# Feed-forward activation tiles at a pitch of 272 columns in place of 264

## The reference

```python
x = x + swiglu_half_ffn(x, ffn1_norm, ffn1_w_in, ffn1_w_out)
h = rms_norm(x, mix_norm)
proj = h @ w_in                       # RWKV-7 part, attention part, branch gates
...
merged = g_a * (o_a @ w_branch_rwkv) + g_b * (o_b @ w_branch_attn)
x = x + merged @ w_out
x = x + swiglu_half_ffn(x, ffn2_norm, ffn2_w_in, ffn2_w_out)

def swiglu_half_ffn(x, norm_g, w_in, w_out):
    h = rms_norm(x, norm_g)
    gate, up = jnp.split(h @ w_in, 2, axis=-1)
    return 0.5 * ((jax.nn.silu(gate) * up) @ w_out)
```

## Time and profile before

| | |
|---|---|
| median of 3 runs | 2350.49 us |
| the profiled execution's span | 2349.0 us |
| TensorE matmul busy | 2337.7 us, 23152 matmuls |
| TensorE weight load busy | 2305.6 us |
| VectorE busy | 1459.5 us |
| ScalarE busy | 985.4 us |
| GpSimd busy | 88.0 us |
| read from HBM | 415.21 MB, 186 GB/s over the span |

### The profile page before, as it was taken

The page is one execution under the profiler, slowest core; times in us unless marked ns, Lnnn a source line. Parts: engine busy times, 40 slices in busy tenths (PEclk is TensorE's granted clock), DMA queues, the critical chain, the costliest instruction groups (busy, mean ns, idle before and its releaser), DMA issues.

```text
span 2349.0 us, 57542 instructions
## 1 busy us (share of the span) xinstructions
PE 2337.7 (100%) x23152; PEld 2305.6 (98%) x23152; DVE 1459.5 (62%) x2004; ACT 985.4 (42%) x1268; POOL 88.0 (4%) x146
## 2 busy tenths in 40 slices
PE   9999999999999999999999999999999999999999
PEld 8999999999999999999999999999999999999999
DVE  6555455555556678878666767766555555545554
ACT  6333333333334544565222346544343333333333
POOL 0000000000002100000000000120000000000000
PEclk9999999999999999999999999999999999999999
DMA  7666566555555756445323637655555555555555
GB/s 240 202 228 209 182 219 245 179 181 182 182 172 170 236 191 208 155 135 187 104 93 114 217 116 209 220 184 183 179 181 184 180 179 179 187 180 180 182 167 171
DMA packets 124082, 428.27 MB, mean 182 GB/s; under 512 B 14488, under 2 KB 20760, under 8 KB 123424
## 3 DMA queue, kind: packets, MB, share of 16 engines
q1 hardware_dynamic: 117504, 393.49, 51.8%
q0 software_dynamic: 6432, 32.64, 4.2%
HBM read 415.21 MB, written 21.33 MB: 186 GB/s over the span
## 4 chain that ended last, share of the span: by engine, by line
PE 96%; DMA 1%; DVE 1%; ACT 1%; issue 0%; DVEq 0%; SPq 0%; ACTq 0%
PE bank L272 30%; PE bank L273 30%; PE bank L274 30%; PE bank L1257 3%; DMA raw<-in_weights 1%; DVE wlo L245 0%; ACT whi L239 0%; DMA x<-in_x 0%; PE bank L1582 0%; PE bank L1395 0%; PE bank L1299 0%; PE bank L1371 0%; PE bank L1598 0%; PE bank L1388 0%; PE bank L1474 0%
## 5 line engine op out<-in xcount | busy, mean ns | idle before, releaser
L245 DVE TENSOR_TENSOR wlo<-raw,whi 128x1024 fp32r<-128x1024 f32 (+3 forms) x794 | 914.0, 1155 | 603.6 <-ACT whi L239 601.2
L272 PE MATMUL bank<-hhi,whi 128*128 128x264 f32 x4048 | 1163.4, 287 | 3.2 <-DVE wlo L245 2.9
L239 ACT ACTIVATE whi<-raw 128x1024 fp32r<-128x1024 f32 (+3 forms) x794 | 793.3, 1002 | 882.6 <-PE bank L274 864.3
L273 PE MATMUL bank<-hlo,whi 128*128 128x264 f32 x4048 | 1147.4, 283 | 0.0
L274 PE MATMUL bank<-hhi,wlo 128*128 128x264 f32 x4048 | 1146.1, 283 | 0.0
L272 PEld LDWEIGHTS bank<-hhi,whi 128*128 128x128 f32 x4048 | 762.5, 188 | 15.4 <-issue 7.3
L273 PEld LDWEIGHTS bank<-hlo,whi 128*128 128x128 f32 x4048 | 763.0, 188 | 0.9
L274 PEld LDWEIGHTS bank<-hhi,wlo 128*128 128x128 f32 x4048 | 759.2, 188 | 0.0
L272 PE MATMUL bank<-mhi,whi 128*128 128x264 f32 x1408 | 399.5, 284 | 0.0
L274 PE MATMUL bank<-mhi,wlo 128*128 128x264 f32 x1408 | 398.9, 283 | 0.0
L273 PE MATMUL bank<-mlo,whi 128*128 128x264 f32 x1408 | 398.9, 283 | 0.0
(11 more groups left out here) (274 smaller groups left out, 1675.7 us busy)
## 6 DMA issues: line engine op xcount, KB each, us to landing
raw<-in_weights SPq DMA_DIRECT2D x666, 512.0 KB, 3.4
raw<-in_weights SPq DMA_DIRECT2D x64, 384.0 KB, 3.1
out_skv<-in_cache POOLq DMA_DIRECT2D x16, 512.0 KB, 4.5
raw<-in_weights SPq DMA_DIRECT2D x32, 256.0 KB, 3.5
raw<-in_weights SPq DMA_DIRECT2D x32, 192.0 KB, 2.5
side<-stg POOLq DMA_DIRECT2D x18, 132.0 KB, 3.7
gates<-side POOLq DMA_DIRECT2D x1, 2376.0 KB, 14.5
x<-in_x SPq DMA_DIRECT2D x4, 528.0 KB, 6.9
```

Source lines behind the costliest of these rows:

```text
L239: act.activation(whi[:, u % RING, 0:n], raw[:, u % RING, 0:n], ACT.Copy).then_inc(hi_done, 1)
L245: dve.tensor_tensor(wlo[:, s, 0:n], raw[:, s, 0:n], whi[:, s, 0:n].bitcast(F32), ALU.subtract).then_inc(lo_done, 1)
L272: pe.matmul(bank[:, 0:T], hi, xhi[:, k], start=(k == 0), stop=False)
L273: pe.matmul(bank[:, 0:T], hi, xlo[:, k], start=False, stop=False)
```

## The change

The gated activations `mhi` and `mlo` are allocated with 272 columns a tile (`WIDE = T + 8`, 1088 bytes, 17 x 64), of which the first 264 are used. As both start on a multiple of 64 bytes, every tile of them does. Before, every second tile began 32 bytes past one. `mlo` then starts 512 bytes later than before, `gated`, `silu`, `prod` and `sq` 1024 bytes later. Shapes, instructions, semaphores and DMAs stay as they are.

```diff
+WIDE = T + 8
...
-        mhi, mlo = put("mhi", at_mix, [DT, T], F32R), put("mlo", at_mix + DT * tile, [DT, T], F32R)
-        gated, silu, prod = (put(k, at_mix + (2 * DT + 2 * i) * tile, [2, T]) for i, k in enumerate(("gated", "silu", "prod")))
-        sq = put("sq", at_mix + (2 * DT + 6) * tile, [DT, T])
+        wide = 4 * WIDE
+        mhi, mlo = (put(k, at_mix + i * DT * wide, [DT, WIDE], F32R)[:, :, 0:T] for i, k in enumerate(("mhi", "mlo")))
+        at_f = at_mix + 2 * DT * wide
+        gated, silu, prod = (put(k, at_f + 2 * i * tile, [2, T]) for i, k in enumerate(("gated", "silu", "prod")))
+        sq = put("sq", at_f + 6 * tile, [DT, T])
```

## The result

The changed kernel takes 2358.68 us (median of 7 runs, 2356.31 to 2361.04) against 2350.42 us for the one before (7 runs): ratio 1.0035, 95% interval 1.0024 to 1.0046. The forecast was 2347.6 us, with a range of 2341.5 to 2355.0.

A forecast was written before the change was run, and what follows sets the result against it. The prediction took TensorE's back-to-back matmuls as the bound. Median 2350.5 us less 2.9 us in the down projections, other parts costing nothing, gave 2347.6 us, with a range of 2341.5 to 2355.0.

The forecast's parts named there:

- What bounds the kernel: Whole kernel: TensorE, busy 2337.7 of 2349.0 us, sets the end; only the distance between matmuls matters, here 510.57 us of down stretches.
- Step 1: Down projections: pitch 1088 leaves only offsets 64, 128, 192, 0; 4224 matmuls at 0.70 ns less each, 2.9 us less.
- the two pricings: Down-stage tiles priced by their own offset (2.9 us less, offset 192 at 366 ns) or the next operand's (3.9 us, 357 to 360).
- the slower case: Rival for the down stages: bad offsets between moving and weight tiles add 3.3 to 7.2 us; chance 0.13.
- The table in the prediction: Time of a tile's three matmuls by offset mod 256, in the four long down stretches: 356.8 to 370.9 ns.
- The bounds: Down stages: nearer limits on the sum, 8.2 us less (best single offset) to 7.2 us more (branch stages).
- The dear side: Upper limit for the down stages, from the branch stages' 121.64 and 122.57 ns a matmul: 3.3 and 7.2 us more.
- Steps 2 to 4: Moved small tensors cost none; VectorE's writes of mhi and mlo at most 0.35 us; semaphores, DMAs, instructions and order unchanged.
- No effect: Rival: the down-stage cycle is paced by something else, offsets only shift time among neighbours, time stays 2350.5 us; chance 0.20.
- A larger gain: Rival: without tiles off the boundary, down-stage tiles fall toward 119.0 ns a matmul, 7.9 us less, 2342.6; chance 0.25.
- The 35 us: Down stages: up to this much to win if all 8.4 ns above the skill's 112.5 ns a matmul were alignment.
- Slower: Rival: moving-tile and weight reads meet at bad offsets in the down stages, +0.77 to +1.70 ns each, 2353.8 to 2357.7; chance 0.13.

The follow-up runs named there:

- e1: Kernel before with mhi, mlo at pitch 1280, each down stage at one offset (0, 64, 128, 32, 96, 192): 123.33, 120.00, 121.33, 121.67, 120.00, 120.95 ns a matmul.
- e3: Against the kernel before: first part pitch 1088, bases 32 bytes on, 121.67 ns a matmul; second part old tiles, small tensors moved 8192 bytes, 92.82 us a long stretch.
- e2: Kernel before at pitch 1280, mhi/mlo both 160, both 224, then 64/192, 64/128, 64/96, 128/64: 122.22, 126.67, 121.48, 122.22, 120.00, 122.22 ns a matmul.
- e9: Kernel before with mhi and mlo at pitch 1280, offset 64 in all six down stages: 2347.05 us, ratio 0.9987.
- e8: Kernel before with wlo 128 bytes on against whi, and mlo 128, 192, 32 bytes on from mhi at pitch 1056: 2361.11 us.

## Why the prediction was wrong

- *What bounds the kernel.* Right: the span moved by 7.6 us and the down stretches by 7.75.
- *Step 1, the sum.* The step that failed is "if each tile keeps the price of its offset". It was tested before the prediction only on one order, that of `hhi` and `mhi`, which pass through the eight offsets in the same sequence. That both agreed to 0.4 ns showed that the address counts; it could not show that an offset has a price of its own. In the new order all four offsets (64, 128, 192, 0) have other prices (369, 366, 363, 375), and e1 gives three of the four others still (360, 364, 363, 370). Forecast -0.70 ns a matmul, measured +1.83: 7.75 us over 4224 matmuls. The tile that was to choose between the two pricings, offset 192, cost 363 ns and fits neither 366 nor 357 to 360. The long stretches passed the 93.4 us that the prediction had set as the sign of the slower case (94.29).
- *What the trace of before already held.* Its 12-tile stages visit the same offsets, but jump from 160 back to 64 at a block's end. There tile 0 costs 369 ns and tile 8 361, both at offset 64; tiles 3 and 11, both at 160, cost 369 and 363. The timeline of one such block, the first matmuls of tiles 0 and 1, then of tiles 8 and 9 (0.37 and 0.36 us apart, rounded to 10 ns):

```profile
718.63 0.28 PE L272 MATMUL bank<-mhi,whi 128*128 128x264 f32 x1
...
719.00 0.29 PE L272 MATMUL bank<-mhi,whi 128*128 128x264 f32 x1
...
721.54 0.28 PE L272 MATMUL bank<-mhi,whi 128*128 128x264 f32 x1
...
721.90 0.29 PE L272 MATMUL bank<-mhi,whi 128*128 128x264 f32 x1
```

  A price per offset fails there by 8 ns a tile. The table in the prediction was made from the four long stages alone.
- *Small slips in the sum.* 4224 x 0.70 is 2.96, not 2.9. The 69.65 us of a short stretch hold 575 distances, so the mean there is 121.1 ns and not 120.92. Together they would have made the gain 3.2 us in place of 2.9.
- *The bounds.* The dear side was cut too short. The branch stages (+0.77 and +1.70 ns) were taken as its end, and the change went just past, +1.83, though the placements tried later reach from 120.00 to 126.67 ns. The range stopped at 2355.0, in the lower half of the slower case, which had a chance of 0.13.
- *Steps 2 to 4.* Right. The small tensors cost nothing (e3, second part), and `mhi` and `mlo` are written in 297 to 304 and 432 to 436 ns.
- *No effect.* Its reason, a rhythm paced by something that ignores the offsets, is refuted by the spread of e1 and e2. The 16-byte line in the Trainium skill (SBUF — State Buffer, Specifications) doesn't cover this: every placement tried is a multiple of 16.
- *A larger gain.* Wrong for this layout. Where a gain does come, in e9, the cause is not that the tiles off a 64-byte boundary are gone: at offset 96 all are off it, and e1 has 120.00 ns there too. The 35 us that the prediction works out by the Trainium skill (TensorE: Matmul & The Clock Gate, Back-to-back issue gap) were no price for this stream: that section gives its formula for an isolated matmul and says that in a stream with a weight load for each matmul both operations set the spacing. No stream here had a steady mean under 120.00 ns.
- *Slower.* The right rival: sign, place and the part of the weights hold; its price, at most 2357.7 us, fell 1 us short of 2358.68. That moving only the weights takes the change's own layout from 94.29 to 93.00 us a stretch is shown. That the two reads meet in the memory is one reading of it; that a weight load's own pace depends on its address is another, and no run here separates them. The Trainium skill (TensorE: Matmul & The Clock Gate, Step-by-step: what each phase is for) has it that the two operands have independent read ports and loading weights takes nothing from the running matmul. The measured dependence on the weights' address (122.78 to 121.11 ns) speaks against that as a full account, but doesn't refute it while the second reading stands.

So the cause is shown as far as this: the place of `mhi` and `mlo` against the weights, and nothing else that the change moved, made the down stages slower. Left open is the rule by which a cycle of offsets settles into its rhythm. The same cycle gave 122.78, 121.11 and 120.55 ns by where it was entered and where the weights lay, and e8's up stages two values at one placement. No run here forecast 122.78 from other measurements.

## What to carry to other kernels

When TensorE is the bound and its stream has no holes, the place of the moving tiles against the weight tiles is a tuning knob of its own (in the down stages here from 0.7% better to 4.8% worse than before; 0.13% of the whole kernel in e9), and it doesn't follow alignment: measure several offsets, one stage each, in one kernel. A price read per position in a periodic stream belongs to the whole sequence; it must not be carried over to another order without a run that has that order, and a stretch of the same trace where the sequence breaks is a first test. A layout that holds the offset still (a pitch that is a multiple of 256 bytes, high and low tiles at one offset) kept all tiles of a stage within 2 ns of one another, and gave the same mean in all seven stages that had offset 0 and all seven that had 64, with the weights at 128. Then the offset can be chosen.

## What the runs showed that was not expected

- The distance of 128x264 fp32r matmuls at the 2.4 GHz level runs from 120.00 to 126.67 ns by where their operands lie and how the stream comes to them.
- 120.00 ns was the lowest steady mean of all placements (offsets 64, 96, 64/96 with weights at 128; four more with weights moved), though single intervals of 115 and 116 ns occur in the cycles.
- A stream at fixed addresses can settle at 120.83 or at 121.39 ns and stay there for more than a thousand matmuls.
- At offsets that never change, tiles can still cost 365, 378 and 350 ns in turn (e2, 64/192).
